# A gated delta rule recurrence on one Trainium2 core: output products grouped by tile form, Y's turns and the query scaling moved, finer waits

## The reference

```python
def gated_delta_rule_chunked(q, k, v, g, beta):      # 8 heads of 128, chunks of C = 64: 4 chunks
    ...
    sol = lax.linalg.triangular_solve(L + eye, rhs, ...)
    u, w = sol[..., :dv], sol[..., dv:]
    A_qk = jnp.einsum('bhnid,bhnjd->bhnij', q, k) * gamma
    q_g = q * jnp.exp(g)[..., None]
    ...
    def step(S, inp):
        u_i, w_i, qg_i, kg_i, A_i, gl_i = inp
        v_new = u_i - jnp.einsum('bhck,bhkv->bhcv', w_i, S)
        o = jnp.einsum('bhck,bhkv->bhcv', qg_i, S) + jnp.einsum('bhij,bhjv->bhiv', A_i, v_new)
        S = S * jnp.exp(gl_i)[..., None, None] + jnp.einsum('bhck,bhcv->bhkv', kg_i, v_new)
        return S, o
```

## Time and profile before

| | us |
|---|---|
| median of 3 runs | 2590.21 |
| lowest and highest run | 2588.77, 2599.34 |
| the profiled execution, its own time | 2588.78 |
| its span | 2587.1 |
| PE busy in the span | 2494.5 (96%) |
| DVE busy | 1469.0 (57%) |
| ACT busy | 1114.3 (43%) |

### The profile page before, as it was taken

The page is one execution under the profiler, slowest core; times in us unless marked ns, Lnnn a source line. Parts: engine busy times, 40 slices in busy tenths (PEclk is TensorE's granted clock), DMA queues, the critical chain, the costliest instruction groups (busy, mean ns, idle before and its releaser), DMA issues.

```text
span 2587.1 us, 58060 instructions
## 1 busy us (share of the span) xinstructions
PE 2494.5 (96%) x24757; PEld 2449.4 (95%) x24757; DVE 1469.0 (57%) x1657; ACT 1114.3 (43%) x1095; POOL 71.5 (3%) x70
## 2 busy tenths in 40 slices
PE   6999979989899999999999899999899999999999
PEld 6999968869899999999999899999899999999999
DVE  5447597654544444444444556675557676765444
ACT  3334434443444444443334344354445555554332
POOL 1000050001000000000000000001000000000000
PEclk8999989989999999999999899999999999999999
DMA  5555400115455555566664466544455555556664
GB/s 171 190 190 193 141 7 4 36 67 163 148 194 195 195 192 190 189 193 194 195 187 122 163 214 227 196 147 147 146 195 195 191 189 190 193 194 195 193 192 151
DMA packets 171475, 431.57 MB, mean 167 GB/s; under 512 B 17711, under 2 KB 23484, under 8 KB 170204
## 3 DMA queue, kind: packets, MB, share of 16 engines
q1 hardware_dynamic: 170123, 422.30, 50.8%
q10 hardware_dynamic: 1232, 7.52, 0.8%
HBM read 427.59 MB, written 2.17 MB: 166 GB/s over the span
## 4 chain that ended last, share of the span: by engine, by line
PE 89%; DVE 8%; ACT 2%; issue 1%; SPq 0%; DMA 0%; POOL 0%; DVEq 0%; ACTq 0%; POOLq 0%
PE ps L1803 27%; PE ps L1804 27%; PE ps L1805 27%; DVE LOW L982 1%; PE ps L1843 1%; DVE NSQ L1016 1%; ACT HIW L554 1%; PE ps L1949 1%; DVE H_ROWS L1024 0%; PE ps L2186 0%; PE ps L2187 0%; DVE TM L1235 0%; DVE LO L1239 0%; DVE TT L1236 0%; DVE CV L1269 0%
## 5 line engine op out<-in xcount | busy, mean ns | idle before, releaser
L982 DVE TENSOR_TENSOR LOW<-RAW,HIW 128x2048 fp32r<-128x2048 f32 (+2 forms) x400 | 910.1, 2275 | 977.6 <-ACT HIW L554 977.4
L1803 PE MATMUL ps<-H_ROWS,HIW 128*128 128x256 f32 x4928 | 1370.4, 278 | 37.9 <-DVE LOW L982 15.5
L1804 PE MATMUL ps<-H_ROWS,HIW 128*128 128x256 f32 x4928 | 1369.4, 278 | 0.0
L1805 PE MATMUL ps<-H_ROWS,LOW 128*128 128x256 f32 x4928 | 1368.2, 278 | 0.0
L554 ACT ACTIVATE HIW<-RAW 128x2048 fp32r<-128x2048 f32 (+2 forms) x400 | 761.3, 1904 | 1180.1 <-PE ps L1805 1176.1
L1803 PEld LDWEIGHTS ps<-H_ROWS,HIW 128*128 128x128 f32 x4928 | 931.8, 189 | 42.0 <-issue 21.5
L1805 PEld LDWEIGHTS ps<-H_ROWS,LOW 128*128 128x128 f32 x4928 | 932.0, 189 | 0.0
L1804 PEld LDWEIGHTS ps<-H_ROWS,HIW 128*128 128x128 f32 x4928 | 931.2, 189 | 0.0
L1803 PE MATMUL ps<-HID,HIW 128*128 (+1 forms) x1408 | 388.7, 276 | 1.3 <-DVE LOW L982 1.3
L1804 PE MATMUL ps<-HID,HIW 128*128 (+1 forms) x1408 | 388.6, 276 | 0.0
L1805 PE MATMUL ps<-HID,LOW 128*128 (+1 forms) x1408 | 388.6, 276 | 0.0
(11 more groups left out here) (351 smaller groups left out, 1533.0 us busy)
## 6 DMA issues: line engine op xcount, KB each, us to landing
RAW<-in_ffn_w_up SPq DMA_DIRECT2D x264, 512.0 KB, 4.6
RAW<-in_ffn_w_down SPq DMA_DIRECT2D x176, 512.0 KB, 4.8
RAW<-in_w_in SPq DMA_DIRECT2D x96, 512.0 KB, 4.2
RAW<-in_fox_w_in SPq DMA_DIRECT2D x96, 512.0 KB, 4.4
RAW<-in_ffn_w_gate SPq DMA_DIRECT2D x88, 512.0 KB, 3.9
RAW<-in_w_out SPq DMA_DIRECT2D x32, 512.0 KB, 5.3
RAW<-in_fox_w_out SPq DMA_DIRECT2D x32, 512.0 KB, 4.9
INV<-rows_out ACTq DMA_DIRECT2D x4, 1024.0 KB, 7.7
```

The costliest lines, as they stand in the source:

```text
L982: V.tensor_tensor(LOW[:, u_const % 4, 0:n], RAW[:, u_const % 4, 0:n], HIW[:, u_const % 2, 0:n].bitcast(F32), ALU.subtract).then_inc(lo_mad ...
L1803: mm(o_, hi_w, h_hi, start=start, stop=False)
L1804: mm(o_, hi_w, h_lo, start=False, stop=False)
L1805: i = mm(o_, lo_w, h_hi, start=False, stop=stop)
```

## The change

Nothing is computed otherwise; the order of the work, the banks, the places of two tiles and the waits change.

- **Outputs** (new function `outputs`): the eight products of the queries with the state come first, then the eight of A with the new values, in the same bank. Only the first product of the bank has `start=True`. The banks are now 7 and 4 (`O_BANKS`), the state sums' 1 and 5 (`STATE_BANKS`), the turned outputs' 6 and 3 (`TURN_BANKS`), those of Y's turns 2, 6, 3 and again 2 (`Y_BANKS`).
- **PE's order ahead of the recurrence**: U products, W products of chunks 0 and 1 (without a wait for `y_gated`), state sums and outputs of chunk 0 (after three `u0_out`), W products of chunks 2 and 3, Y's turns 0 and 1, W times the state of chunk 1, Y's turns 2 and 3, state sums of chunk 1, and on.
- **DVE**: the queries are scaled first, as soon as ACT has taken the exponential, now right behind the inversion's last level on ACT, ahead of the copies to U0. The copies to WT stand on either side of the first state. The gating of Y (four `heads_gated`, two `heads_full`) goes between the recurrence's own steps.
- **ACT**: the high part of BON is rounded in two halves of 1024 elements, behind the scaled outputs of chunks 0 and 1. DVE's low part of each waits for it.
- **Places**: the state's second buffer lies where the unscaled queries were (so the first state waits for `q_grown`), and SD moves.

The core of the diff:

```diff
+STATE_BANKS, O_BANKS, TURN_BANKS, Y_BANKS = (1, 5), (7, 4), (6, 3), (2, 6, 3, 2)
@@ ACT @@
+                if lev == 5:
+                    act.wait_ge(S("rows_landed"), 80)
+                    A(QG[:], QG[:], ACT.Exp).then_inc(S("g_rows_exp"), 1)
...
-            act.wait_ge(S("rows_landed"), 80)
-            A(QG[:], QG[:], ACT.Exp).then_inc(S("g_rows_exp"), 1)
...
-                if c == 1:
-                    got("ya_full", 2)
-                    A(H(0, 0, PAIRS), BON[:], ACT.Copy).then_inc(S("mix_hi"), 1)
...
                 o_scaled(c)
+                if c < 2:
+                    got("ya_full")
+                    A(H(0, 4 * c, 4 * c + 4), BON[:, 4 * c:4 * c + 4, :], ACT.Copy).then_inc(S("mix_hi"), 1)
@@ DVE @@
+            queries_grown()
+            weights_out(0)
+            weights_out(1)
+            got("q_grown")
+            state_added(0)
             state_decayed(1)
+            weights_out(2)
+            weights_out(3)
+            heads_gated(0)
+            heads_gated(1)
             got("u0_out", 4)
 
             values_made(1)
-            queries_grown()
             o_variance(0)
+            heads_full(0)
             settle()
             state_added(1)
             o_inverse(0)
             state_decayed(2)
+            heads_gated(2)
+            heads_gated(3)
+            heads_full(1)
+
+            values_made(2)
+            o_variance(1)
             got("mix_hi")
             heads_low(0)
-
-            values_made(2)
-            o_variance(1)
             settle()
             state_added(2)
             o_inverse(1)
             o_gated(0)
+            got("mix_hi")
             heads_low(1).then_inc(S("mix_made"), 1)
@@ PE @@
+            def outputs(c, vn):
+                o_ = ps[O_BANKS[c % 2]]
+                for a in range(G_QK if c else 0):
+                    for e, rr in enumerate(halves_of):
+                        mm(o_[rr, a * P:(a + 1) * P], QG[:, 2 * a + e, c * C:(c + 1) * C], gS[c % 2][:, 4 * e + a, :],
+                           start=a == 0, stop=False, skip_group_check=True)
+                for a in range(G_QK):
+                    for rr in halves_of:
+                        ins = mm(o_[rr, a * P:(a + 1) * P], AL[rr, c, a, 0, :], vn[rr, a, :], start=c == 0 and a == 0, stop=True,
+                                 skip_group_check=True)
+                ins.then_inc(S("o_summed"), 1)
+
+            chunk_weights(0)
+            got("u0_out", 3)
+            state_sums(0, U0[:, 0, :, :])
+            outputs(0, U0[:, 0, :, :])
+            chunk_weights(2)
+            got("y_normed")
+            got("wt_out", 2)
+            turned_heads(0)
+            turned_heads(1)
+            got("u0_out")
+            for c in range(1, NCH):
...
+                ins.then_inc(S("ws_summed"), 1)
+                if c == 1:
+                    got("wt_out", 2)
+                    turned_heads(2)
+                    got("y_gated")
+                    turned_heads(3)
+                else:
+                    got("y_gated", 2 if c == 2 else 1)
+                    turned_values(c - 2)
+                got("vn_made")
+                if c < NCH - 1:
+                    state_sums(c, vn)
                 if c == 1:
                     got("q_grown")
...
+                outputs(c, vn)
```

More of the change, by code:

```diff
@@ L801, in o_scaled @@
                 for a in range(G_QK):
-                    ins = A(OT[:, c, a, :], ps[3 + c % 2][:, a * P:(a + 1) * P], ACT.Copy, scale=MS[:, c, a:a + 1])
+                    ins = A(OT[:, c, a, :], ps[O_BANKS[c % 2]][:, a * P:(a + 1) * P], ACT.Copy, scale=MS[:, c, a:a + 1])
                 ins.then_inc(S("o_out"), 1)
@@ L1413, in heads_gated @@
                 got("y_turned")
-                V.tensor_tensor(GATE[:, f2, :], GATE[:, f2, :], pair_of(SIDE_BANKS[e]), ALU.mult).then_inc(S("y_gated"), 1)
+                V.tensor_tensor(GATE[:, f2, :], GATE[:, f2, :], pair_of(Y_BANKS[e]), ALU.mult).then_inc(S("y_gated"), 1)
             def heads_full(half):
@@ L1419, in heads_full, with weights_out @@
                 V.tensor_tensor(BON[:, f4, :], BON[:, f4, :], GATE[:, f4, :], ALU.add).then_inc(S("ya_full"), 1)
-            for e in range(4):
-                heads_gated(e)
-            for k in range(4):
+            def weights_out(k):
                 e, c2 = k % 2, 2 * (k // 2)
@@ L1434, in state_added @@
                     if c == 0:
-                        V.tensor_copy(after[:, h4, :], bank(1 + hb)).then_inc(S("gs_out"), 1)
+                        V.tensor_copy(after[:, h4, :], bank(STATE_BANKS[hb])).then_inc(S("gs_out"), 1)
                     else:
-                        V.tensor_tensor(after[:, h4, :], SD[:, h4, :], bank(1 + hb), ALU.add).then_inc(S("gs_out"), 1)
+                        V.tensor_tensor(after[:, h4, :], SD[:, h4, :], bank(STATE_BANKS[hb]), ALU.add).then_inc(S("gs_out"), 1)
             def state_decayed(c):
@@ L2126, in _, with turned_heads @@
             got("tokens_scaled", 4)
-            got("y_normed")
-            for e in range(4):
+            def turned_heads(e):
                 for t in (2 * e, 2 * e + 1):
@@ L2141, in _, with chunk_weights @@
                 ins.then_inc(S("u0_summed"), 1)
-            for c2 in (0, 2):
-                pe.wait_ge(S("y_gated"), c2 + 2)
+            def chunk_weights(c2):
                 for c in (c2, c2 + 1):
@@ L2157, in turned_values, with state_sums @@
                 for a in range(G_QK):
[L2158 removed]
+                    ins = mm(ps[TURN_BANKS[c % 2]][:, a * P:(a + 1) * P], OT[:, c, a, :], ident[:], start=True, stop=True)
                 ins.then_inc(S("o_turned"), 1)
[L2161 to L2175 removed]
+            def state_sums(c, vn):
+                for a in range(G_QK):
@@ L2176, in _ @@
                     for e, rr in enumerate(halves_of):
-                        ins = mm(ps[1 + e][:, a * P:(a + 1) * P], KG[rr, c, a, :], vn[rr, a, :], start=True, stop=True)
+                        ins = mm(ps[STATE_BANKS[e]][:, a * P:(a + 1) * P], KG[rr, c, a, :], vn[rr, a, :],
+                                 start=True, stop=True)
                         if a == G_QK - 1:
                             ins.then_inc(S("gs_summed"), 1)
+            def outputs(c, vn):
[4 more added lines that the diff above has]
+                           start=a == 0, stop=False, skip_group_check=True)
+                for a in range(G_QK):
+                    for rr in halves_of:
+                        ins = mm(o_[rr, a * P:(a + 1) * P], AL[rr, c, a, 0, :], vn[rr, a, :], start=c == 0 and a == 0, stop=True,
+                                 skip_group_check=True)
+                ins.then_inc(S("o_summed"), 1)
@@ new lines, in _ @@
+            chunk_weights(0)
[9 more added lines that the diff above has]
+            for c in range(1, NCH):
+                vn = VN[:, c % 2, :, :]
+                got("gs_out", 2)
+                for a in range(G_QK):
+                    for e, rr in enumerate(halves_of):
+                        ins = mm(ps[0][rr, a * P:(a + 1) * P], WT[:, c, e, a, :], gS[c % 2][:, 4 * e + a, :],
+                                 start=True, stop=True)
+                ins.then_inc(S("ws_summed"), 1)
[10 more added lines that the diff above has]
+                    state_sums(c, vn)
@@ L2180, in _ @@
                 if c == 1:
                     got("q_grown")
-                for a in range(G_QK):
-                    for e, rr in enumerate(halves_of):
-                        o_ = ps[3 + c % 2][rr, a * P:(a + 1) * P]
-                        if c:
-                            mm(o_, QG[:, 2 * a + e, cc], s0[:, 4 * e + a, :], start=True, stop=False)
-                        ins = mm(o_, AL[rr, c, a, 0, :], vn[rr, a, :], start=c == 0, stop=True)
-                ins.then_inc(S("o_summed"), 1)
+                outputs(c, vn)
```

31 lines of the change are left out of this document (5 added, 26 removed).

## The result

The changed kernel takes 2570.86 us (median of 6 runs, 2567.64 to 2578.93), the kernel before 2590.93 (median of 6, 2588.54 to 2599.34). The ratio is 0.9924, with a 95% interval of 0.9911 to 0.9937, so between 16 and 23 us less; the medians lie 20.1 apart. Predicted were 2573.3 us, 16.9 less.

The account below looks back on a forecast made before the run. PE bounds the kernel, busy 2494.5 of 2587.1 us. Terms 5.0 + 7.7 + 0.4 + 3.6 - 1.5 + 3.6 - 1.8 give 17.0 us less, the walk itself 16.9: 2590.2 - 16.9 = 2573.3 us, range 2567 to 2580.

Parts of the forecast that it names:

- The walk: Recurrence up to the projection, new order stepped through with the old durations: projection starts at 565.7, 16.9 us earlier.
- Chunk 1's outputs: Recurrence, chunk 1: outputs start at 542.1, 5.0 us earlier, and take 2.2 us for 9.9, 7.7 less.
- Chunk 2's: Recurrence, chunk 2: outputs from 549.4 to 551.6, 3.6 us less; the stretch ahead of them 0.4 less.
- Chunk 3's: Recurrence, chunk 3: outputs from 555.2 to 557.4, 3.6 us less; the stretch ahead of them 1.5 more.
- the tail: From the last outputs to the projection: ACT and DVE come late, 8.3 us for 6.5, 1.8 more.
- The step on the form: Outputs: alternating forms is what costs; grouped, a step takes 2.2 us for 5.8 (high clock) or 9.9 (low).
- B: Outputs: form is not the cause, each product costs 0.36 us anywhere; 11.1 us less, 2579.1; chance 0.07.
- A: Recurrence: the clock falls again, low from 545 on; 14.0 us less, 2576.2; chance 0.13.
- E: Tail and chunk 3: tail doesn't lengthen, PE waits less; 19 to 20 us less, 2571; chance 0.08.
- C: Four new handoffs: DVE and ACT slower than walked, 0.5 to 1 us each; 2575 to 2577; chance 0.13.
- D: Ahead of chunk 1: clock low from 527 on, slower than before, 2592.4; chance 0.04 with the like.
- Nothing moves against it: Behind the projection's start: weights wait in their buffers, order is as before, so no loss there.

Follow-up runs that it names:

- e7: Changed kernel with the high part of the first weights split off on ACT in chunk 0 instead of chunk 2; 2577.24 us, one run.
- e3: Changed kernel with query and A products alternating but shifted by two, so none adds to the sum its neighbour just wrote; 2578.07 us, one run.
- e1: Kernel before with only the outputs grouped by form, in the old place, banks and order; 2575.31 us, ratio 0.9942.
- e4: Changed kernel with outputs in runs of two: two query products, then two A products, and so on; 2568.26 us, one run.
- e5: Changed kernel with outputs grouped by form, but within each form four products of one half, then four of the other; 2573.48 us, one run.
- e10: Changed kernel with DVE and ACT reordered: new values earlier, tail by need, first weights split behind chunk 0's scaled outputs; 2570.66 us, ratio 0.9914.
- e2: Changed kernel with the outputs alternating again (query product, A product), the rest of the change kept; 2581.94 us, ratio 0.9964.
- e9: The changed kernel itself, unaltered, measured once more; 2575.74 us, ratio 0.9923.

## Why the prediction was right

**The walk.** It has to be read 1.3 us later, since the changed kernel's trace came to the stretch so much later (526.06 for 524.78). Chunk 1's outputs: walked 542.1, so 543.4; measured 543.49. Chunk 2's: 549.4, so 550.7; measured 550.40. Chunk 3's: 555.2, so 556.5; measured 555.98. The walk said where PE would wait and for what, 1.5 us each for DVE's new values; it is 1.29 (1.49 for the weight load) and 1.35. That part of the sum was right term by term, to within 0.3 us each. One reading in it was not: of the 7.7 us for chunk 1's outputs it put 4.1 on the clock. Grouped, two runs at the low clock take 3.7 us (1.86 and 1.81 in e7), so only 1.6 of the 7.7 hang on the clock; the sum is the same.

**The term that was mis-sized is the tail.** I had 8.3 us from the end of the last outputs to the projection; it is 6.9 (558.02 to 564.91). 0.9 of the difference is the last turn, which I had put at the low clock (2.08); it takes 1.16, the clock falls only behind it. The other 0.5 is ACT and DVE, which had done the squares and the variance of chunk 3 about 1 us ahead of the walk, while the outputs were 0.7 ahead. Of that 0.7 the output steps are 0.5, 2.04 us for my 2.2, three times. These make the 2.1 us between 16.9 and 19.0: the chain of small steps was walked too slow, not wrongly.

**The step on the form was right in sum, wrong in its parts.** "It is the form that costs" holds against the rival that the sum in one bank costs (e3), and B is out by e1 and the changed kernel's rows. But the change of form is only 0.15 to 0.19 us of the 0.36, and 0.06 to 0.11 is that a lone product has no neighbour on the other half (e4, e5). The rows from which I concluded that it is the form could not tell the two apart: there each row holds two products, one on either half. Nor were they "twice the work", since two products of 64 columns have as many columns as one of 128. For the price of full grouping this made no difference, since I took it from a row of a whole run; for any other grouping it did, as e4 and e5 showed. The Trainium skill (TensorEngine Tiling (Array Packing), "Tiling Modes") states that changing the tiling mode drains TensorE; the 0.15 to 0.19 us for a change of form agree with that. The rule of the same skill that spoke against the change (TensorE: Matmul & The Clock Gate, "Part 3: Packing small matmuls"), that a load over the same row group never overlaps, is not what the traces show: eight products over all 128 rows take 1.02 us with 0.85 us of weight loads beside them, where the rule, priced with the lone product, gives 8 x 0.36. Even four in a row on the same half stay below it (e5, eight in 1.51). The same part of the skill also lets a load run ahead when it goes to the background weight buffer, which the prediction left out; no run here shows where the loads went. That it would hardly have mattered is seen too: e4's steps of 2.94 us cost 0.2 us in the stretch, as the walk had said of longer ones.

**The clock.** A didn't happen: PE was busy for 3.47 of 5 us and 3.27 of 5, and the clock stayed at 1.00. It fell where PE was busy for 1.25 of 5. But the comparison on which A rested doesn't hold: in e10 the clock stayed at 1.00 from 555 to 560 with PE busy for 2.32 of 5 us, less than the 2.61 ahead of the fall in the kernel before. I had seen that chunk 1's outputs ran at the low clock and counted 4.1 us for it. What I had not seen is that the alternation itself went with its staying low so long (e1).

**The other rivals.** What came is E's number, 19 to 20 us less and 2571, and not C's: the new places cost less than walked, and PE's waits were 0.2 us shorter each. E's reason was half right: the tail did lengthen, from 6.5 to 6.9 us, if only by 0.4. D had its test in the earlier trace rows against the rows of the changed kernel: from 535 to 545 PE is busy without a gap, where before it was busy for 6.1 of 10 us.

**Behind the projection.** "Nothing moves against it" was not quite so. The projection's low clock lasts longer in the changed kernel, from 564.91 to 570.6 against 582.61 to 585.9 before, but at HID nothing of it is left: 19.2 us less, counted from the start of the stretch. Behind 1152 us the program varies by up to 9 us between executions of one kernel, more than anything that could still be hidden there.

## What to carry to other kernels

Where TensorE's products are small, order them so that neighbours have one form and lie on different halves: runs of two already give most of it (a step of 2.94 us, against 5.8 alternating and 2.04 grouped), and a lone product costs 0.36 us where one in a run costs 0.13. When a recurrence passes through several engines, walk it with the measured durations, every engine's queue in its order; the walk was right to about half a us at each chunk, and it also says how much of a saving the next wait will swallow. And a gain ahead of a chain of small steps (square, root, reciprocal, scale, turn) is worth only what that chain lets through: order the tail by who is waited for, before shortening what leads to it.

## What the runs showed of the hardware

- A run of n float32 products of 128 columns, of forms 128*64 or 64*64 that take turns on two halves, costs, by a fit, 0.15 us for the change of form and 0.22 for each pair (0.36, 0.37, 0.58 and 1.02 us for one, two, three and eight, in e2, e4, e3 and the changed kernel). With four on one half and then four on the other it is 0.17 a product (e5, 1.51 us for eight). At the low clock one takes 0.62 and eight 1.86 (in e7, 558.32 to the start of the next run at 560.18), so about 0.2 for the change and 0.41 a pair.
- With alternating forms the clock stayed at its lower level for all of their ten us (before, 547 to 557), with PE's rows covering that time, and it rose some 5 us behind them; grouped, with the same 2 us of idle time ahead, it was up again within 3.5 us of that idle time's end (e1). At the high level the same alternation did not lower it (e2, 1.00 from 535 to 570). A busy PE in the rows is not yet one that brings the clock back. Why the lone products don't is open: no run took the form apart from the pairing at the low clock.
- The same code behind the stretch took 2003.0 us in one execution and 2012.3 in another (changed kernel and e9); the difference arises between 1152 and 1916 us, in part at a granted clock of 1.00 in both.
